# The rotary key projection as one chunk: weights held, x moving, result turned back by TensorE

## The chip, the cores and the metric

The kernel runs on one core of a Trainium2 chip. TensorE (PE) does matrix products and transposes into PSUM, VectorE (DVE) and ScalarE (ACT) work element by element, GpSimd (POOL) does small tables and issues some DMAs, SyncE (SP) issues the weight loads. The metric is the device time in microseconds of one execution, as the median of several runs.

## The reference, cut to what matters

Two decoder layers over 256 tokens of width 2048. Layer 0 is attention with a combined input projection, layer 1 a state-space (S5) layer; each is followed by layer norm, a gated feed-forward part and another layer norm. The part around the change:

```python
q_lat, kv_lat, k_pe, qd, kd, vd = jnp.split(h @ w_in, splits, axis=-1)   # k_pe: 64 columns
q = (_rmsnorm(q_lat, q_norm) @ w_q_b).reshape(B, S, MLA_HEADS, NOPE_DIM + ROPE_DIM)
q = jnp.concatenate([q[..., :NOPE_DIM], _rope(q[..., NOPE_DIM:], positions)], axis=-1)
kv = (_rmsnorm(kv_lat, kv_norm) @ w_kv_b).reshape(B, S, MLA_HEADS, NOPE_DIM + V_DIM)
k_pe = jnp.broadcast_to(_rope(k_pe[:, :, None, :], positions), (B, S, MLA_HEADS, ROPE_DIM))
k = jnp.concatenate([kv[..., :NOPE_DIM], k_pe], axis=-1)
```

So k_pe is x (256 x 2048) times a weight of 2048 x 64, rotated by position, and shared by the eight heads.

## The kernel before, in words

All weights come as "chunks" of two row tiles (2 x 128 rows) and up to 512 columns, 512 KB each. SP loads them one after the other into a ring of four slots, `RAW` (`load`, L250 to L256); a load waits until DVE is done with the chunk four before it (`lo_ready`). A product in full f32 is made of three in fp32r: ACT copies the chunk to `WH`, which keeps the high part (`hi`, L689), DVE writes the rest to `WL` (`lo`, L974), and PE adds up x_hi w_hi, x_hi w_lo and x_lo w_hi (`chunk`, L349 to L351). `hi` and `lo` of chunk c wait until PE has used chunk c - 4 (`w_used`); PE waits for `lo_ready`. In `chunk` a tile of x (128 rows by 128 tokens) is the stationary operand and the weights, 512 columns, are the moving one; the result has the tokens on the partitions. There are 12 matmuls a chunk, 2 row tiles x 2 token tiles x 3.

Each engine runs its own program, whose order is written out by hand and tied together by semaphores. `PHASES` gives each projection its number of blocks, the chunks of a block, the number of its first chunk and of its first block. Blocks alternate between two accumulators `A` in PSUM (`acc_ready` waits for `acc_free`).

The order around the change is: "win" (8 blocks of 8 chunks, chunks 0 to 63), "kpe" (one block, chunks 64 to 71, of width 64, so that each matmul writes 128 x 64 and loads 128 x 128 of x), "qb" (3 blocks of 2 chunks), "kvb" (4 blocks of 2 chunks), then attention, then "wout". In the kpe phase ACT splits five narrow chunks, copies out the last block of win (`win_end(7)`, L725) and splits the other three. DVE, after the first two chunks of qb, waits for the end of kpe, rotates the result straight from PSUM into `STG` (`rotate`, L1032 to L1034, six operations), writes it twice side by side (L1102) and counts `staged`, for which PE's `turn_up(0)` waits. That turns it by two transposes (L414), and DVE copies the turned key to `KP` (`whole_turned`, L986). `Y`, two banks of PSUM, lies unused in this stage.

Of the kernel before, what the change touches and what calls it, by code (L numbers as in the profile page):

```python
# [25 lines left out]
P = 128  # L26
TOK = 256
TT = TOK // P
D = 2048
KT = D // P  # L30
WB = 512
RING = 4
# [3 lines left out]
ROPE = 64  # L36
# [16 lines left out]

PHASES = {}
_c = _b = 0
for _name, _n, _per in [("win", 8, 8), ("kpe", 1, 8), ("qb", 3, 2), ("kvb", 4, 2), ("wout", 4, 8),
                        ("ple0", 4, 1), ("gate0", 4, 8), ("inA0", FA, 8), ("outA0", 4, FA), ("inB0", FB, 8), ("outB0", 4, FB),
                        ("glu", 8, 8),
                        ("ple1", 4, 1), ("gate1", 4, 8), ("inA1", FA, 8), ("outA1", 4, FA), ("inB1", FB, 8), ("outB1", 4, FB)]:
    PHASES[_name] = (_n, _per, _c, _b)  # L60
    _c += _n * _per
    _b += _n if not _name.startswith("ple") else 0
# [20 lines left out]
def build(nc, t, out):  # L83
# [3 lines left out]
    with ExitStack() as ctx:  # L87
# [3 lines left out]
        def sem(name):  # L91
            return ctx.enter_context(nc.semaphore(name))


        RAW = at("raw", [P, RING, 2, WB], 0)
# [94 lines left out]
        turn_done = sem("turn_done")  # L190
        turn_hi = sem("turn_hi")
        turned = sem("turned")
        staged = sem("staged")
        v_step = sem("v_step")
        sq_sum = sem("sq_sum")
        trig = sem("trig")
# [22 lines left out]
        n = 0  # L219
# [21 lines left out]
        def _(sp):  # L241
# [16 lines left out]
            def phase(name, weight, width=WB, first=0):  # L258

                nb, per, c0, _ = PHASES[name]  # L260
                w, total = t[weight], nb * per
                if c0 == 0:
                    for j in range(first):
                        load(w, j, j, 0, None, width)
                        if j < 2:
                            load_x(2 + j)
                if (total - first) % RING:
                    for j in range(first, total):
                        load(w, j, c0 + j, 0, None, width)
                elif total - first == RING:  # L270
                    for j in range(first, total):
                        load(w, j, c0 + j, 0, None, width)
                else:
                    with sp.Fori(0, (total - first) // RING) as i:
                        for j in range(RING):
                            load(w, first + j, c0 + first + j, RING, i, width)
# [41 lines left out]
                    sp.dma_start(TS[n % 10][:], c_dram[n].rearrange("p (a c n) -> p a c n", a=4, c=2)).then_inc(ts_in[n % 10], 16)  # L318

            phase("win", "w_in", first=RING)  # L320
            phase("kpe", "w_kpe", ROPE)
            phase("qb", "w_qb")
            phase("kvb", "w_kvb")
            phase("wout", "w_out")
# [15 lines left out]
        def _(pe):  # L340
            def chunk(c, coef, i, hi, lo, kt, depth, acc, width=WB):

                pe.wait_ge(lo_ready, lin(c + 1, coef, i))
                s = c % RING
                for k in range(2):
                    for q in range(TT):
                        cols = slice(q * P, (q + 1) * P)
                        o = A[:, acc, q, 0:width]
                        pe.matmul(o, hi[:, kt + k, cols], WH[:, s, k, 0:width], start=(kt + k == 0), stop=False)  # L349
                        pe.matmul(o, hi[:, kt + k, cols], WL[:, s, k, 0:width], start=False, stop=False)  # L350
                        last = pe.matmul(o, lo[:, kt + k, cols], WH[:, s, k, 0:width], start=False,  # L351
                                         stop=(kt + k == depth - 1))
                last.then_inc(w_used, 1)
# [28 lines left out]
            for b in range(8):  # L382
                acc_ready(b0 + b)
                for j in range(per):
# [8 lines left out]
                    if j == 3 and 1 <= b <= 6:  # L393
                        pe.wait_ge(staged, b)
                        first = TG["lat"] + 2 * (b - 1) if b <= 2 else TG["qk"] + 2 * (b - 3)
                        for g in range(2):
                            turn(first + g, STG[:, (b - 1) % 2], 256 * g)
            _, per, c0, b0 = PHASES["kpe"]
            acc_ready(b0)
            for j in range(per):  # L400
                chunk(c0 + j, 0, None, XH, XL, 2 * j, KT, b0 % 2, ROPE)


            QB, KVB = PHASES["qb"], PHASES["kvb"]
# [1 line left out]

            def turn_up(m):

                pe.wait_ge(staged, 7 + m)
                if m == 0:  # L410
                    g = TG["kpe"]
                    pe.wait_ge(turned, g - 1)
                    for q in range(TT):
                        last = pe.transpose(TP[:, g % 2, 0, q * P:(q + 1) * P], STG[:, 0, q, 0:P], ID[:])  # L414
                    last.then_inc(turn_done, 1)
                else:
                    for g in range(2):
                        turn(groups[m] + g, STG[:, m % 2], 256 * g)

            pe.wait_ge(turned, TG["qk"])  # L420
            for b in range(7):
                acc_ready(QB[3] + b)
                for j in range(2):
                    row = 2 * j
                    part = slice(0, 4) if b < 3 else slice(4, 8)
                    chunk(QB[2] + 2 * b + j, 0, None, LH[:, part], LL[:, part], row, 4, (QB[3] + b) % 2)
                if b >= 1 and b <= 6:
                    turn_up(b - 1)

# [243 lines left out]
        def _(act):  # L673
# [9 lines left out]
            def hi(c, coef=0, i=None, width=WB):  # L683

                s = c % RING
                act.wait_ge(raw_full[s], lin(16 * (c // RING + 1), 16 * coef // RING, i))
                if c >= RING:
                    act.wait_ge(w_used, lin(c - RING + 1, coef, i))
                act.activation(WH[:, s, :, 0:width], RAW[:, s, :, 0:width], ACT.Copy).then_inc(hi_ready, 1)  # L689
# [20 lines left out]
            def win_end(b):  # L710

                end("win", b)
                if b < 2:
                    if b == 0:
                        act.wait_ge(const_in, 6 * 16)
                    else:
                        act.wait_ge(sq_sum, 2 * b)
                    for q in range(TT):
                        act.activation(GTf[:, WB * q:WB * (q + 1)], A[:, b % 2, q], ACT.Square,
                                       accum_out=SC[:, 2 * b + q:2 * b + q + 1]).then_inc(sq_sum, 1)  # L720
                elif b < 6:
                    act.wait_ge(turn_done, TG["lat"] + 2 * (b - 1))
                    act.activation(STG[:, b % 2], A[:, b % 2], ACT.Copy).then_inc(staged, 1)
                else:
                    act.activation(VD[:, :, (b - 6) * WB:(b - 5) * WB], A[:, b % 2], ACT.Copy).then_inc(acc_free, 1)  # L725
# [17 lines left out]
                            n_ = 2 * (b - 1) + g  # L743
                            hi_turned(TG["lat"] + n_, LH[:, 2 * n_:2 * n_ + 2, :])
            c0 = PHASES["kpe"][2]
            for j in range(8):
                hi(c0 + j, width=ROPE)
                if j == 4:
                    win_end(7)
            QB, KVB = PHASES["qb"], PHASES["kvb"]  # L750

            def up_end(m):
# [206 lines left out]
        def _(dve):  # L959
# [8 lines left out]
            def lo(c, coef=0, i=None, width=WB):  # L968

                s = c % RING  # L970
                dve.wait_ge(hi_ready, lin(c + 1, coef, i))
                if c >= RING:
                    dve.wait_ge(w_used, lin(c - RING + 1, coef, i))
                dve.tensor_tensor(WL[:, s, :, 0:width], RAW[:, s, :, 0:width], WH[:, s, :, 0:width].bitcast(F32),  # L974
                                  ALU.subtract).then_inc(lo_ready, 1)
# [99 lines left out]
                                n_ = 2 * (b - 3) + g  # L1075
                                whole_turned(TG["qk"] + n_, QK[:, 2 * n_:2 * n_ + 2, :])
            c0 = PHASES["kpe"][2]
            for j in range(8):
                lo(c0 + j, width=ROPE)
            QB = PHASES["qb"]  # L1080

            def up_turned(m):
# [9 lines left out]
            for b in range(7):  # L1092
                lo(QB[2] + 2 * b)
                lo(QB[2] + 2 * b + 1)
                if b == 0:

                    end("kpe", 0)
                    src = A[:, PHASES["kpe"][3] % 2, :, 0:ROPE].rearrange("p t (h c n) -> p t h c n", h=1, c=2)
                    dve.wait_ge(turn_done, TG["kpe"])
                    dst = STG[:, 0, :, 0:ROPE].rearrange("p t (h c n) -> p t h c n", h=1, c=2)  # L1100
                    link(rotate(src, dst, 1))
                    link(dve.tensor_copy(STG[:, 0, :, ROPE:2 * ROPE], STG[:, 0, :, 0:ROPE]))  # L1102
                    dve.nop().then_inc(staged, 1)
                    dve.nop().then_inc(acc_free, 1)
                if b in (1, 2, 4, 5):
                    dve.wait_ge(staged, 7 + b)
                    dve.nop().then_inc(acc_free, 1)
                if b == 3:
                    end("qb", 2)
                    dve.wait_ge(turn_done, TG["qn"] + 2)  # L1110
                    src = A[:, (QB[3] + 2) % 2].rearrange("p t (h c n) -> p t h c n", h=HEADS, c=2)
                    dst = STG[:, 1].rearrange("p t (h c n) -> p t h c n", h=HEADS, c=2)
                    link(rotate(src, dst, HEADS))
                    dve.nop().then_inc(staged, 1)
                    dve.nop().then_inc(acc_free, 1)
                if b >= 2:
                    up_turned(b - 2)
# [814 lines left out]
```

## Time and profile before

| | us |
|---|---|
| median of 3 runs | 2473.98 (2472.92 to 2474.0) |
| the profiled execution | 2473.81 |
| its span | 2472.0 |
| PE busy | 2340.4 |
| DVE busy | 1453.1 |
| ACT busy | 1033.2 |
| mean granted clock of PE, of full | 0.971 |

The span is the time from the first to the last instruction of the profiled execution. Busy times of the engines overlap. The durations of neighbouring matmuls overlap too, since they are pipelined; how fast PE goes is read from the distance of their starts. The granted clock has two levels here, 2.4 GHz (1.00) and 1.2 GHz (0.50); a value between them for a stretch is a mean.

### The profile page before, as it was taken

To read this page: it belongs to the slowest core of one execution; us is meant where nothing else is said; L and a number is where in the kernel's file an instruction comes from. 1 tells how busy PE (TensorE), PEld (TensorE's weight loads), DVE (VectorE), ACT (ScalarE), POOL (GpSimd) and SP (SyncE) were. 2 spreads that over 40 slices of the span, in tenths; PEclk is the share of its full clock that TensorE was granted. 3 is DMA by queue.
4 is the path that set the end of the run, shared out by engine and by line. 5 is a ranking of instruction groups with operands and counts; after the bars stand their busy time and mean duration, and the time that the engine had idled before them with its cause. 6 is when DMAs were issued, how large, how long until landed. Compare 5 with 4: busy or idle time off the path is not lost.

```text
span 2472.0 us, 32904 instructions
## 1 busy us (share of the span) xinstructions
PE 2340.4 (95%) x10996; PEld 1927.8 (78%) x10996; DVE 1453.1 (59%) x1924; ACT 1033.2 (42%) x1134; POOL 219.3 (9%) x327
## 2 busy tenths in 40 slices
PE   8999999999999999999948499989999999999996
PEld 6888687888888888888836488868888888888885
DVE  5544757666667776557836755475544444445455
ACT  4443544444444334444333044344444443444442
POOL 0000048501111011101210000000000000000000
PEclk9998999999999999999969799999999999999998
DMA  6554264768787667767685156556555555555553
GB/s 237 186 181 128 87 198 144 234 222 259 256 266 251 227 232 240 240 196 253 228 196 171 51 183 195 171 181 196 192 187 189 189 191 194 191 191 189 188 189 117
DMA packets 136992, 483.02 MB, mean 195 GB/s; under 512 B 18656, under 2 KB 19168, under 8 KB 135744
## 3 DMA queue, kind: packets, MB, share of 16 engines
q1 hardware_dynamic: 121568, 429.44, 53.7%
q0 software_dynamic: 14048, 50.80, 6.8%
q10 hardware_dynamic: 1280, 1.48, 0.2%
q8 instruction: 62, 1.02, 0.2%
q14 instruction: 34, 0.28, 0.0%
HBM read 457.80 MB, written 19.14 MB: 193 GB/s over the span
## 4 chain that ended last, share of the span: by engine, by line
PE 91%; DVE 5%; DMA 2%; issue 1%; ACT 1%; DVEq 0%; SPq 0%; ACTq 0%
PE ps L349 28%; PE ps L350 28%; PE ps L351 28%; PE ps L365 1%; PE ps L628 1%; PE ps L589 1%; DMA h_quarter<-res 1%; DVE w_lo L974 1%; DVE gated L1549 1%; DMA raw<-in_w_in 1%; DVE gated L1547 1%; DMA raw<-in_w_glu 1%; DVE res L1202 0%; ACT w_hi L689 0%; PE ps L448 0%
## 5 line engine op out<-in xcount | busy, mean ns | idle before, releaser
L974 DVE TENSOR_TENSOR w_lo<-raw,w_hi 128x1024 fp32r<-128x1024 f32 (+1 forms) x782 | 951.8, 1220 | 859.7 <-ACT w_hi L689 856.7
L689 ACT ACTIVATE w_hi<-raw 128x1024 fp32r<-128x1024 f32 (+1 forms) x782 | 822.1, 1053 | 1190.3 <-PE ps L351 1152.0
L349 PE MATMUL ps<-w_hi,x_hi 128*128 128x512 f32 (+1 forms) x2336 | 917.0, 393 | 17.9 <-DVE x_lo L982 14.8
L351 PE MATMUL ps<-w_hi,x_lo 128*128 128x512 f32 (+1 forms) x2336 | 910.9, 390 | 0.0
L350 PE MATMUL ps<-w_lo,x_hi 128*128 128x512 f32 (+1 forms) x2336 | 910.5, 390 | 0.0
L349 PEld LDWEIGHTS ps<-w_hi,x_hi 128*128 128x128 f32 x2336 | 442.8, 190 | 109.9 <-DVE x_lo L982 16.7
L351 PEld LDWEIGHTS ps<-w_hi,x_lo 128*128 128x128 f32 x2336 | 442.6, 189 | 91.4
L350 PEld LDWEIGHTS ps<-w_lo,x_hi 128*128 128x128 f32 x2336 | 443.0, 190 | 88.4
L349 PE MATMUL ps<-w_hi,hid_hi 128*128 128x512 f32 x704 | 275.2, 391 | 0.0
L350 PE MATMUL ps<-w_lo,hid_hi 128*128 128x512 f32 x704 | 274.1, 389 | 0.0
L351 PE MATMUL ps<-w_hi,hid_lo 128*128 128x512 f32 x704 | 274.0, 389 | 0.0
L349 PEld LDWEIGHTS ps<-w_hi,hid_hi 128*128 128x128 f32 x704 | 132.1, 188 | 28.7 <-issue 1.4
L351 PEld LDWEIGHTS ps<-w_hi,hid_lo 128*128 128x128 f32 x704 | 132.2, 188 | 27.8
L350 PEld LDWEIGHTS ps<-w_lo,hid_hi 128*128 128x128 f32 x704 | 132.2, 188 | 27.0
L1643 POOL TENSOR_TENSOR s_small<-s_small 64x128 f32<-64x128 f32 x93 | 71.1, 764 | 7.5
L628 PE MATMUL ps<-s_table,states 128*64 128x128 f32 x256 | 32.1, 290 | 39.3 <-DVE states L1551 39.3
L628 PEld LDWEIGHTS ps<-s_table,states 128*64 128x64 f32 x256 | 30.9, 198 | 39.9 <-DVE states L1551 39.5
L577 PE MATMUL ps<-ident,h_steps 64*128 64x64 f32 x64 | 7.8, 314 | 33.8 <-ACT h_steps L894 33.8
L1764 POOL DMA_DIRECT2D s_e_dram<-s_e x16 | 8.9, 558 | 338.2 <-DVE s_e L1342 338.2
L921 ACT ACTIVATE z<-ps 128x512 f32<-128x512 f32 x8 | 4.8, 598 | 81.6 <-PE ps L628 81.6
L1757 POOL DMA_DIRECT2D s_coef<-s_coef_dram x64 | 35.5, 561 | 4.4 <-DMA s_coef_dram<-s_small 4.2
L1261 DVE TENSOR_TENSOR gated<-ps,gated 128x512 f32<-128x512 f32 x44 | 30.2, 685 | 8.5 <-ACT gated L856 8.5
(201 smaller groups left out, 1339.7 us busy)
## 6 DMA issues: line engine op xcount, KB each, us to landing
raw<-in_w_inA SPq DMA_DIRECT2D x192, 512.0 KB, 4.3
raw<-in_w_inB SPq DMA_DIRECT2D x160, 512.0 KB, 4.1
raw<-in_w_outA SPq DMA_DIRECT2D x96, 512.0 KB, 4.3
raw<-in_w_outB SPq DMA_DIRECT2D x80, 512.0 KB, 4.3
raw<-in_w_in SPq DMA_DIRECT2D x64, 512.0 KB, 4.1
raw<-in_w_gate SPq DMA_DIRECT2D x64, 512.0 KB, 4.3
raw<-in_w_glu SPq DMA_DIRECT2D x64, 512.0 KB, 4.3
raw<-in_w_out SPq DMA_DIRECT2D x32, 512.0 KB, 4.3
```

The costliest lines, as they stand in the source:

```text
L349: pe.matmul(o, hi[:, kt + k, cols], WH[:, s, k, 0:width], start=(kt + k == 0), stop=False)
L350: pe.matmul(o, hi[:, kt + k, cols], WL[:, s, k, 0:width], start=False, stop=False)
L351: last = pe.matmul(o, lo[:, kt + k, cols], WH[:, s, k, 0:width], start=False, stop=(kt + k == depth - 1))
L365: last = pe.transpose(TP[:, g % 2, k, q * P:(q + 1) * P], src[:, q, col + k * P:col + (k + 1) * P], ID[:])
L589: last = pe.matmul(PS[0:SLOTS, 2 * (tile % 2) + a // 2, TOK * (a % 2):TOK * (a % 2 + 1)], U4[:, 4 * tile + a, :], TS[tile % 6][:, a].rearr ...
L628: last = pe.matmul(bank_of(pair), ST[:, :, ri, pair], TS[n_ % 10][:, a, ri, :], start=False, stop=(ri == 1), skip_group_check=True)
L689: act.activation(WH[:, s, :, 0:width], RAW[:, s, :, 0:width], ACT.Copy).then_inc(hi_ready, 1)
L974: dve.tensor_tensor(WL[:, s, :, 0:width], RAW[:, s, :, 0:width], WH[:, s, :, 0:width].bitcast(F32), ALU.subtract).then_inc(lo_ready, 1)
L1261: dve.tensor_tensor(GT[:, 1], A[:, bb % 2, :, 256:512], GT[:, 0], ALU.mult).then_inc(hid_ready, 1)
L1547: ins = dve.tensor_tensor(prod[h], abar[:, :, :, m], x.unsqueeze(1).broadcast_to([P, 2, 2, half]), ALU.mult)
L1643: link(pool.tensor_tensor(o, a, b, op))
L1757: pool.dma_start(EC[n][PW * s:PW * (s + 1)].rearrange("p a c n -> p a (c n)"), src).then_inc(e_raw[n], 16)
```

## The change

kpe becomes one chunk of 512 KB that holds all 16 row tiles of the 2048 x 64 weight. Its slices of 64 columns are the stationary operand, and x_hi or x_lo, 256 tokens wide, is the moving one: 16 x 3 = 48 matmuls that write 64 x 256, features on the partitions. DVE copies that to a free part of `STG`, PE transposes it back by two transposes into `Y` after the first chunk of qb (`turn_kpe`), and DVE rotates from there, now after the splits of qb's chunks 3 and 4. The rotations count a semaphore of their own, `rotated`, and the numbers that `staged` is waited for are shifted. Chunks and blocks after kpe keep their order; their chunk numbers are lower by seven.

```diff
-for _name, _n, _per in [("win", 8, 8), ("kpe", 1, 8), ("qb", 3, 2), ...
+for _name, _n, _per in [("win", 8, 8), ("kpe", 1, 1), ("qb", 3, 2), ...
             phase("win", "w_in", first=RING)
-            phase("kpe", "w_kpe", ROPE)
+            c = PHASES["kpe"][2]
+            sp.wait_ge(lo_ready, c - RING + 1)
+            sp.dma_start(RAW[:, c % RING].rearrange("p k n -> p (k n)").rearrange("p (a n) -> p a n", a=KT // 2),
+                         t["w_kpe"].rearrange("a p n -> p a n")).then_inc(raw_full[c % RING], 16)
...
             acc_ready(b0)
-            for j in range(per):
-                chunk(c0 + j, 0, None, XH, XL, 2 * j, KT, b0 % 2, ROPE)
+            pe.wait_ge(lo_ready, c0 + 1)
+            w_hi, w_lo = (w[:, c0 % RING].rearrange("p k n -> p (k n)") for w in (WH, WL))
+            for k in range(KT):
+                o, cols = A[0:ROPE, b0 % 2, 0, 0:TOK], slice(ROPE * k, ROPE * (k + 1))
+                pe.matmul(o, w_hi[:, cols], XH[:, k, :], start=(k == 0), stop=False)
+                pe.matmul(o, w_lo[:, cols], XH[:, k, :], start=False, stop=False)
+                last = pe.matmul(o, w_hi[:, cols], XL[:, k, :], start=False, stop=(k == KT - 1))
+            last.then_inc(w_used, 1)
+
+            def turn_kpe():
+
+                pe.wait_ge(kpe_out, 1)
+                for q in range(TT):
+                    first = WB // 2 + q * P
+                    last = pe.transpose(Y[:, 0, ROPE * q:ROPE * (q + 1)], STG[0:ROPE, 0, 1, first:first + P], ID[0:ROPE, 0:ROPE])
+                last.then_inc(kpe_turned, 1)
...
             def turn_up(m):
 
-                pe.wait_ge(staged, 7 + m)
+                if m in (0, 3):
+                    pe.wait_ge(rotated, m // 3 + 1)
+                else:
+                    pe.wait_ge(staged, 6 + m if m < 3 else 5 + m)
...
                     chunk(QB[2] + 2 * b + j, 0, None, LH[:, part], LL[:, part], row, 4, (QB[3] + b) % 2)
+                    if b == 0 and j == 0:
+                        turn_kpe()
...
             c0 = PHASES["kpe"][2]
-            for j in range(8):
-                hi(c0 + j, width=ROPE)
-                if j == 4:
-                    win_end(7)
+            hi(c0)
+            win_end(7)
...
             c0 = PHASES["kpe"][2]
-            for j in range(8):
-                lo(c0 + j, width=ROPE)
+            lo(c0)
...
                 if b == 0:
-
                     end("kpe", 0)
-                    src = A[:, PHASES["kpe"][3] % 2, :, 0:ROPE].rearrange("p t (h c n) -> p t h c n", h=1, c=2)
                     dve.wait_ge(turn_done, TG["kpe"])
+                    dve.tensor_copy(STG[0:ROPE, 0, 1, WB // 2:WB], A[0:ROPE, PHASES["kpe"][3] % 2, 0, 0:TOK]).then_inc(kpe_out, 1)
+                    dve.wait_ge(kpe_out, 1)
+                    dve.nop().then_inc(acc_free, 1)
+                if b == 1:
+                    dve.wait_ge(kpe_turned, 1)
+                    src = Y[:, 0, 0:TT * ROPE].rearrange("p (t h c n) -> p t h c n", t=TT, h=1, c=2)
                     dst = STG[:, 0, :, 0:ROPE].rearrange("p t (h c n) -> p t h c n", h=1, c=2)
                     link(rotate(src, dst, 1))
                     link(dve.tensor_copy(STG[:, 0, :, ROPE:2 * ROPE], STG[:, 0, :, 0:ROPE]))
-                    dve.nop().then_inc(staged, 1)
-                    dve.nop().then_inc(acc_free, 1)
+                    dve.nop().then_inc(rotated, 1)
                 if b in (1, 2, 4, 5):
-                    dve.wait_ge(staged, 7 + b)
+                    dve.wait_ge(staged, 6 + b if b < 3 else 5 + b)
```

## Rows read from the trace of the kernel before

**Rows 1.** The page: PE's busy line, and the chain that ended last by engine.

```profile
PE 2340.4 (95%) x10996; PEld 1927.8 (78%) x10996; DVE 1453.1 (59%) x1924; ACT 1033.2 (42%) x1134; POOL 219.3 (9%) x327
...
PE 91%; DVE 5%; DMA 2%; issue 1%; ACT 1%; DVEq 0%; SPq 0%; ACTq 0%
```

**Rows 2.** Busy time by stretches, around kpe; columns in the first line.

```profile
core 0: us, PE busy (x) PEld busy (x) DVE busy (x) ACT busy (x) POOL busy (x), PEclk, DMA share, GB/s
...
199.93:205.20 5.27, 5.27 (x49) 5.26 (x48) 1.17 (x4) 2.15 (x5) 0.00 (x0) 1.00 0.42 123
205.20:215.44 10.24, 10.24 (x50) 10.24 (x50) 2.74 (x3) 3.48 (x4) 0.00 (x0) 0.50 0.74 240
215.44:218.90 3.46, 3.46 (x9) 2.78 (x10) 2.70 (x8) 1.06 (x1) 0.00 (x0) 0.50 0.09 37
```

**Rows 3.** PE in order of time: start, duration, line, out<-in, stationary, out.

```profile
199.93 0.19 PE L349 MATMUL ps<-w_hi,x_hi 128*128 128x64 f32 x1
...
205.21 0.40 PE L349 MATMUL ps<-w_hi,x_hi 128*128 128x64 f32 x1
...
215.44 0.77 PE L349 MATMUL ps<-w_hi,lat_hi 128*128 128x512 f32 x1
...
218.95 0.39 PE L351 MATMUL ps<-w_hi,lat_lo 128*128 128x512 f32 x1
```

**Rows 4.** Weight loads of L349 (0 to 460 us) and L589: ns minimum/median/maximum.

```profile
L349 PEld LDWEIGHTS ps<-w_hi,x_hi x470: 186/188/333, 12.0 to 459.9; 128*128 128x128 f32 x157
...
L589 PEld LDWEIGHTS ps<-s_table,u x128: 132/137/231, 1293.8 to 1333.9; 128*64 128x64 f32 x128
```

**Rows 5.** An S5 stage with 64 weight columns: PE's order, and a stretch.

```profile
1299.86 1.94 PE L589 MATMUL ps<-s_table,u 128*64 128x256 f32 x8
1301.73 0.71 PE L603 MATMUL ps<-ident,e_slots 64*128 64x64 f32 x8
...
1300.00:1310.00 10.00, 10.00 (x65) 6.30 (x65) 4.04 (x4) 4.03 (x5) 0.00 (x0) 1.00 0.72 218
```

**Rows 6.** PE in order of time around two transposes of L414.

```profile
227.79 0.40 PE L351 MATMUL ps<-w_hi,lat_lo 128*128 128x512 f32 x1
228.03 0.38 PE L414 MATMUL ps<-ident,stage 128*128 128x128 f32 x2
...
228.48 0.39 PE L350 MATMUL ps<-w_lo,lat_hi 128*128 128x512 f32 x1
```

**Rows 7.** ACT and DVE in order of time; in brackets idle time before and releaser.

```profile
189.31 1.06 ACT L689 ACTIVATE w_hi<-raw 128x1024 fp32r<-128x1024 f32 x1 [1.66 <-PE ps L351]
192.03 0.31 ACT L689 ACTIVATE w_hi<-raw 128x128 fp32r<-128x128 f32 x1 [1.66 <-PE ps L351]
...
201.67 1.01 ACT L725 ACTIVATE v_dil<-ps 128x1024 f32<-128x1024 f32 x1
...
190.40 1.23 DVE L974 TENSOR_TENSOR w_lo<-raw,w_hi 128x1024 fp32r<-128x1024 f32 x1 [1.49 <-ACT w_hi L689]
...
215.67 0.23 DVE L1032 TENSOR_TENSOR gated<-ps,cos_sin 128x64 f32<-128x64 f32 x1 [2.75 <-PE ps L351]
...
229.67 0.42 DVE L986 COPY k_pe<-ps 128x256 f32<-128x256 f32 x1 [2.53 <-ACT stage L762]
```

**Rows 8.** SP's issues of kpe, and DMA issues with us to landing.

```profile
183.64 17.91 SPq L256 DMA_DIRECT2D raw<-in_w_kpe  x8
...
raw<-in_w_in SPq DMA_DIRECT2D x4, 512.0 KB, 4.0
...
raw<-in_w_kpe SPq DMA_DIRECT2D x8, 64.0 KB, 2.2
```

**Rows 9.** PE in attention, the same step of three heads in order of time.

```profile
282.87 1.22 PE L465 MATMUL ps<-probs_t,v_dil 128*128 128x256 f32 x2
...
287.92 0.70 PE L465 MATMUL ps<-probs_t,v_dil 128*128 128x256 f32 x2
...
290.99 0.70 PE L465 MATMUL ps<-probs_t,v_dil 128*128 128x256 f32 x2
```

More of the change, by code:

```diff
@@ L55 @@
 _c = _b = 0
-for _name, _n, _per in [("win", 8, 8), ("kpe", 1, 8), ("qb", 3, 2), ("kvb", 4, 2), ("wout", 4, 8),
+for _name, _n, _per in [("win", 8, 8), ("kpe", 1, 1), ("qb", 3, 2), ("kvb", 4, 2), ("wout", 4, 8),
                         ("ple0", 4, 1), ("gate0", 4, 8), ("inA0", FA, 8), ("outA0", 4, FA), ("inB0", FB, 8), ("outB0", 4, FB),
@@ L192, in build @@
         turned = sem("turned")
-        staged = sem("staged")
+        staged, rotated, kpe_out, kpe_turned = sem("staged"), sem("rotated"), sem("kpe_out"), sem("kpe_turned")
         v_step = sem("v_step")
@@ L397, in _ @@
                             turn(first + g, STG[:, (b - 1) % 2], 256 * g)
-            _, per, c0, b0 = PHASES["kpe"]
+            _, _, c0, b0 = PHASES["kpe"]
             acc_ready(b0)
-            for j in range(per):
-                chunk(c0 + j, 0, None, XH, XL, 2 * j, KT, b0 % 2, ROPE)
+            pe.wait_ge(lo_ready, c0 + 1)
[12 more added lines that the diff above has]
+                last.then_inc(kpe_turned, 1)
             QB, KVB = PHASES["qb"], PHASES["kvb"]
@@ L1113, in _ @@
                     link(rotate(src, dst, HEADS))
-                    dve.nop().then_inc(staged, 1)
+                    dve.nop().then_inc(rotated, 1)
                     dve.nop().then_inc(acc_free, 1)
```

## The prediction

> **What bounds the kernel now.** I read the page first. TensorE (PE) is busy 95% of the span, and the chain that ended last is 91% PE and 5% VectorE (DVE) [rows 1]. So, outside a few places, a microsecond taken from PE's stream is a microsecond of the span, and work of ScalarE (ACT), DVE or the DMA queue matters only where PE comes to wait for it. The granted clock by stretches comes second. The rotary key projection ("kpe") starts at 199.93; PE is busy in all of it, yet from 205.20 its clock is at half rate, 1.2 instead of 2.4 GHz, until 218.90, well into the query projection ("qb") that follows [rows 2]. Third, PE's order of time gives the intervals between starts, which is what counts, since the durations of neighbours overlap [rows 3]:
>
> - 48 of the 96 narrow matmuls (64 columns out) run from 199.93 to 205.21, 0.11 us each; the other 48, at the half clock, from 205.21 to 215.44, 0.213 us each. Together 15.51 us.
> - The first 8 matmuls of qb, of 512 columns, take from 215.44 to 218.95, 3.51 us. At full clock the next 39, up to 227.79 [rows 6], take 8.84 us, 0.2267 each, so those eight would be 1.81 us.
>
> PE has no idle time anywhere in these rows: nobody feeds it too late, it is slow by itself.
>
> **Why narrow matmuls cost so much.** 64 columns at one a cycle are 27 ns of 2.4 GHz, but the interval is 111 ns. Two readings fit. (a) The weight load sets it: each narrow matmul has to load 128 columns of x. A load of 128 columns stands in the trace with a median of 188 ns, one of 64 columns with 137 ns [rows 4], so 64 columns more cost 51 ns and 128 cost some 102, nearly the whole interval. (b) A narrow fp32r matmul streams at a quarter of the wide one's rate: 4 x 64 cycles are 107 ns. Both double at the half clock. I take (a), because of what the clock does: it falls after 5.3 us of this stage although PE shows as busy without a gap [rows 2, 3], as it would with an array that streams in only a quarter of its cycles, and it stays at full in a stage of the S5 layer, where matmuls with 64 weight columns stream 256 columns at length [rows 5].
>
> **The change, part by part.** The sum is made against the profiled execution, 2473.81 us (span 2472.0 and 1.8 around it); the median of the runs is 2473.98, 0.2 above.
>
> 1. *The projection on PE.* 96 matmuls of 64 columns with 128 weight columns each go; 48 come, with 64 weight columns (51 ns of load) and 256 moving. No row has this form in fp32r. Nearest below: the 512-wide ones at 0.2267 us take 544 cycles of 2.4 GHz, so they stream one column a cycle, and 256 columns cannot go below 0.107. Nearest above: the plain-f32 form of the same size, 128x64 weights and 256 columns, one record each 0.234 us (eight from 1299.86 to 1301.73) [rows 5]. I take the lower side, since type and buffers are those of the 512-wide row: its 0.2267 less 512 columns at 2.4 GHz (0.2133) leaves 0.0134 of overhead a matmul, and 0.1067 + 0.0134 = 0.120. 48 x 0.120 = 5.76 us; the bounds are 5.1 and 11.2.
> 2. *The clock.* The new stream fills 256 of 288 cycles, so I expect full rate all through: the eight slow qb matmuls become 1.81 us. The doubt is that only 64 of 128 array columns work; the S5 rows with 64 weight columns stay at 1.00 all the same [rows 5].
> 3. *Turning back.* Two PE transposes are added after qb's first chunk. Two such, from L414, stretch the step from 227.79 to 228.48 to 0.69 us where two matmuls would take 0.45: +0.24 us [rows 6]. The two old transposes of the rotated key stay.
> 4. *Who must be in time for PE.* Weights of kpe: its load is issued at 183.64 as before, when the slot is free [rows 8]. It is one of 512 KB in 1024 pieces of 512 bytes instead of eight of 64 KB in 256 pieces of 256 bytes. The old one lands after 2.2 us and a full chunk in 4 KB pieces after 4.0 [rows 8]; four times 2.2 is 8.8, so it is there by 192.4 at the latest. The ACT copy that may start at 192.03 becomes 1.06 us (189.31) instead of 0.31 and the DVE difference 1.23 (190.40) [rows 7], ending by 194.8; PE wants it at 199.93. Cost nothing, with 5 us of cover, and the loads behind it on SP's queue have more.
>    On ACT, the copy-out of the last "win" block (1.01 us, at 201.67 before [rows 7]) now stands in front of the splits of all qb chunks, and waits for PE's end of win: about 200.2 to 201.2. Then the first qb chunk: ACT to 202.3, DVE to 203.5; the second to 204.7. PE wants the first at 199.93 + 5.76 = 205.7. This is the tightest cover, 2.2 us. It was nothing before, when the narrow stage gave 15.5 us. If it failed, PE would wait at the start of qb by just the difference.
>    On DVE, the new copy PSUM to STG of 64x256 comes after the stage's end, some 205.95; the row of a 128x256 copy says 0.42 us [rows 7], so about 206.4. Behind it on DVE stand the differences of chunks three and four of qb (to 207.7 and 208.9) and PE wants these at 211.4 and later. PE's new wait for that copy stands before qb's second chunk and everything behind it, but is reached only at 208.4: 2.0 us of cover. The accumulator is freed right after the copy, also in time. DVE's wait for the turned key (about 208.9) holds the rotation, six operations and a copy that start at 215.67 now and take 0.23 us each, say 0.25 with what lies between [rows 7], until about 210.8; PE asks for the result only after two more chunks, at 216.9, and DVE's next difference waits for ACT until 213.7 anyway. Nothing.
> 5. *Removed off the path.* Seven small ACT copies and seven small DVE differences, and seven DMA issues. They lie beside a busy PE: nothing gained.
>
> Sum over what is replaced: before 15.51 + 3.51 = 19.02; after 5.76 + 1.81 + 0.24 = 7.81. Gain 11.2 us, 2473.98 - 11.2 = **2462.8 us**. Later work is released by PE's progress, so it all moves earlier; I found no timer of its own: POOL's S5 preparation and the SP loads wait for PE's or DVE's counts.
>
> 5a. *What the Trainium skill would make of it.* "TensorE: Matmul & The Clock Gate", section "LDWEIGHTS (loading the stationary operand)", gives a load as its columns / 1.2 in ns: 107 for 128 columns, 53 for 64. That agrees with the 51 ns step of the rows and with reading (a). The same page, "Back-to-back issue gap", puts a full-clock gap at N/2.4 + 2.5 ns, 109 for 256 columns; as an estimate from it the stage would be 5.2 us and the time 2462.3. Its 216 ns for 512 columns is below the measured 226.7, so I stay with the rows.
>
> **What moves besides.** The stages after this one have low-activity places where the clock falls and recovers. In attention one head takes from 282.87 to 287.92, 5.05 us, at the half clock, and the next one 3.07 to 290.99 [rows 9]. Such dips need not fall on the same heads once all is 11 us earlier. I price that by two heads' difference, 2 x 2 us, as +-4 us on any outcome.
>
> **Rivals.**
>
> A. *The clock falls in the new stage too*, since half the array's columns idle. For: it fell after 5.3 us in the old one, and the new one lasts 5.8. Against: the S5 rows. Price: the last 4 matmuls at double interval +0.4 and qb's start slow as now, +1.7, so 2464.9; if it fell halfway, 24 x 0.107 + 1.7 = 4.3, 2467.1.
>
> B. *256 columns of fp32r at two cycles each*, as a record of the plain-f32 form shows: 0.234 x 48 = 11.2 us, 5.5 more than forecast, 2468.3. For: same shape. Against: another type, and the 512-wide fp32r rows run at one.
>
> C. *Reading (b) holds, and 256 is still "narrow"*: four cycles a column. 0.427 + 0.005 = 0.432 each, 20.7 us; or, by two records of the f32 form, 0.468 and 22.5 us. After: 22.8 to 24.5 against 19.02, 3.7 to 5.5 us slower, 2477.7 to 2479.5. This is the case on the other side; it turns from gain to loss where one matmul costs over (19.02 - 1.81 - 0.24)/48 = 0.354 us. For: the 64-wide interval fits it to 5 ns. Against: the falling clock.
>    "FP8 and Floating Point Precision" of the Trainium skill, section "TensorE Precision Notes", says that true FP32 takes four passes through the array. The rows of the 512-wide fp32r form have one; if the narrow form had four, that is case C with its times.
>
> D. *It doesn't do what it says:* PE waits for a late feed at qb's start and takes back what it won. For: cover there shrinks to 2.2 us. Against: it is still cover; a stall of over 6 us would be needed to reach "no difference". I give it little.
>
> **How the numbers follow.** The forecast, full clock and about 0.12 us each: 74%, 2462.8 with 2458.5 to 2467. A: 10%. B: 5%. C: 5%. D, and dips further on that are worse or better than +-4 us: 6%. The range takes in A, most of B and the lower side of the dips: 2458 to 2468.5, leaving out C, the rest of D and the tails. About 0.2%, 5 us, is what a measurement of this kernel can tell from no change. Faster by more: 74 + 10 + 4 of B + 3 of the rest = 0.91. Within: 1 of B, 2 of C, 3 of the rest = 0.06. Slower by more: 3 of C = 0.03.
>
> **What would show it.** In the profile of the changed kernel: 48 matmuls 128*64 with 64x256 out, intervals 0.11 to 0.12 and the stage over at about 205.7; a granted clock of 1.00 from 200 to 240; the first qb matmul at 0.23 intervals and no idle time before it; two transposes at about 208.4 with no wait for the DVE copy; the rotation from about 209; qb beginning at 205.7 and everything after it 11 us earlier. An interval of 0.23 shows B, 0.43 or more C; a clock of 0.5 at qb's start A; idle time before qb released by the DVE difference D. If these stand and the total is off by several us, the difference must be found where the clock dips in later stages, and my ignorance of those is what is likeliest to spoil the figure.

## The result

The changed kernel takes 2462.66 us (median of 6 runs, 2458.5 to 2463.01), beside 2473.99 for the kernel before in the same comparison (6 runs, 2469.99 to 2478.03). The ratio is 0.9949, with an interval of 0.9939 to 0.9959: about 0.5% or 12.6 us faster by the ratio, 11.3 by the two medians. The prediction was 2462.8.

The profile after was taken of the quickest of the six executions (2458.5 us, span 2456.7), so it shows more than the change alone. The page of the changed kernel, the lines that answer to [rows 1]:

```profile
span 2456.7 us, 32749 instructions
...
PE 2323.5 (95%) x10950; PEld 1912.6 (78%) x10950; DVE 1452.3 (59%) x1918; ACT 1030.9 (42%) x1127; POOL 220.3 (9%) x327
...
PE 90%; DVE 5%; DMA 2%; issue 1%; ACT 1%; DVEq 0%; SPq 0%; ACTq 0%
```

PE is the bound as before; its busy time fell by 16.9 us, DVE's and ACT's hardly. Next its order of time around kpe, to be held against [rows 3] and [rows 6] (L407 to L409 are the new matmuls, L417 the turning back, L352 to L354 the old `chunk`):

```profile
199.76 0.28 PE L407 MATMUL ps<-x_hi,w_hi 128*64 128x256 f32 x1
...
205.09 0.28 PE L409 MATMUL ps<-x_lo,w_hi 128*64 128x256 f32 x1
205.20 0.40 PE L352 MATMUL ps<-w_hi,lat_hi 128*128 128x512 f32 x1
...
207.04 0.39 PE L354 MATMUL ps<-w_hi,lat_lo 128*128 128x512 f32 x1
...
207.72 0.39 PE L354 MATMUL ps<-w_hi,lat_lo 128*128 128x512 f32 x1
208.04 0.34 PE L417 MATMUL ps<-ident,stage 64*128 64x64 f32 x2
208.31 0.50 PE L352 MATMUL ps<-w_hi,lat_hi 128*128 128x512 f32 x1
208.65 0.39 PE L353 MATMUL ps<-w_lo,lat_hi 128*128 128x512 f32 x1
```

The 48 matmuls take 5.44 us, from 199.76 to 205.20, 0.1133 each, with an even step; the first eight of qb follow in 1.84 us (to 207.04) without idle time. The stretches that answer to [rows 2], with the same columns, show the full clock all through:

```profile
199.90:205.70 5.80, 5.80 (x52) 5.71 (x50) 2.66 (x3) 4.11 (x5) 0.00 (x0) 1.00 0.25 75
205.70:215.00 9.30, 9.30 (x42) 7.41 (x41) 5.67 (x12) 3.75 (x4) 0.00 (x0) 1.00 0.56 179
```

ACT and DVE in order of time, for [rows 7]:

```profile
199.96 1.03 ACT L747 ACTIVATE v_dil<-ps 128x1024 f32<-128x1024 f32 x1 [7.04 <-PE ps L354]
200.88 2.95 ACT L711 ACTIVATE w_hi<-raw 128x1024 fp32r<-128x1024 f32 x3
...
201.96 2.36 DVE L994 TENSOR_TENSOR w_lo<-raw,w_hi 128x1024 fp32r<-128x1024 f32 x2 [7.79 <-ACT w_hi L711]
205.41 0.42 DVE L1117 COPY stage<-ps 64x256 f32<-64x256 f32 x1 [1.08 <-PE ps L409]
206.04 2.36 DVE L994 TENSOR_TENSOR w_lo<-raw,w_hi 128x1024 fp32r<-128x1024 f32 x2 [0.21 <-DVE stage L1117]
208.41 0.22 DVE L1052 TENSOR_TENSOR gated<-ps,cos_sin 128x64 f32<-128x64 f32 x1
```

ACT waits 7.04 us for the end of win and only then begins with qb's chunks, as foreseen; DVE has the first ready near 203.2, 2 us before PE begins with it at 205.20. The copy of the result is done at 205.83, 2.2 us before the transposes. Last, the one load of kpe, beside [rows 8]:

```profile
raw<-in_w_kpe SPq DMA_DIRECT2D x1, 512.0 KB, 4.5
```

Attention starts at 250.94, before at 262.31 (L443's first matmul). Of these 11.37 us the stages ahead of kpe, which the change leaves alone, are 0.17 (199.93 against 199.76); 11.20 are the change's, against the execution before that the rows were read from. Another profile of the kernel before gives more, see the section after the experiments.

### The profile page after: what moved, and what is told of

The parts are those of the page before. It is cut to its first block, busy times and chain, and to the rows that moved or that the text cites. A ratio compares the mean times of both kernels' runs of the same rounds, so it can differ in the third digit from the quotient of the medians.

```text
span 2456.7 us, 32749 instructions
## 1 busy us (share of the span) xinstructions
PE 2323.5 (95%) x10950; PEld 1912.6 (78%) x10950; DVE 1452.3 (59%) x1918; ACT 1030.9 (42%) x1127; POOL 220.3 (9%) x327
## 4 chain that ended last, share of the span: by engine, by line
PE 90%; DVE 5%; DMA 2%; issue 1%; ACT 1%; DVEq 0%; SPq 0%; ACTq 0%
PE ps L352 28%; PE ps L354 28%; PE ps L353 28%; PE ps L368 1%; PE ps L650 1%; PE ps L611 1%; DVE w_lo L994 1%; DMA h_quarter<-res 1%; DMA raw<-in_w_in 1%; DVE gated L1571 1%; DVE gated L1569 1%; DMA raw<-in_w_glu 1%; DVE res L1224 0%; ACT w_hi L711 0%; PE ps L625 0%
## 5 line engine op out<-in xcount | busy, mean ns | idle before, releaser
L994 DVE TENSOR_TENSOR w_lo<-raw,w_hi 128x1024 fp32r<-128x1024 f32 x775 | 950.4, 1229 | 850.1 <-ACT w_hi L711 847.3
L711 ACT ACTIVATE w_hi<-raw 128x1024 fp32r<-128x1024 f32 x775 | 820.4, 1060 | 1173.7 <-PE ps L354 1135.3
L352 PE MATMUL ps<-w_hi,x_hi 128*128 128x512 f32 x2304 | 905.7, 393 | 18.5 <-DVE x_lo L1002 15.1
L354 PE MATMUL ps<-w_hi,x_lo 128*128 128x512 f32 x2304 | 899.4, 390 | 0.0
L353 PE MATMUL ps<-w_lo,x_hi 128*128 128x512 f32 x2304 | 899.0, 390 | 0.0
L352 PEld LDWEIGHTS ps<-w_hi,x_hi 128*128 128x128 f32 x2304 | 434.2, 188 | 109.3 <-DVE x_lo L1002 17.0
L354 PEld LDWEIGHTS ps<-w_hi,x_lo 128*128 128x128 f32 x2304 | 433.9, 188 | 91.4
L353 PEld LDWEIGHTS ps<-w_lo,x_hi 128*128 128x128 f32 x2304 | 434.3, 189 | 88.7
L352 PE MATMUL ps<-w_hi,hid_hi 128*128 128x512 f32 x704 | 275.2, 391 | 0.0
L354 PE MATMUL ps<-w_hi,hid_lo 128*128 128x512 f32 x704 | 274.0, 389 | 0.0
L352 PEld LDWEIGHTS ps<-w_hi,hid_hi 128*128 128x128 f32 x704 | 132.1, 188 | 28.6 <-issue 1.4
L354 PEld LDWEIGHTS ps<-w_hi,hid_lo 128*128 128x128 f32 x704 | 132.2, 188 | 27.7
L1569 DVE TENSOR_TENSOR gated<-a_bar,states 128x128 f32<-128x128 f32 x124 | 32.1, 288 | 5.0 <-ACT states L937 1.9
```

The source lines that it names most:

```text
L1569: ins = dve.tensor_tensor(prod[h], abar[:, :, :, m], x.unsqueeze(1).broadcast_to([P, 2, 2, half]), ALU.mult)
```

## Experiments

The theory, L: a narrow matmul costs the load of its weight columns, and the clock falls because little streams through the array, although PE shows as busy. The rival, S: under some width fp32r streams at a quarter of the rate. The prediction had chosen L on the clock's word; a width of 256 that comes out well fits both, if S's width lies under it.

**Half the moving columns.** `e1_move128`: twice the matmuls, the same loads each.

```diff
-                o, cols = A[0:ROPE, b0 % 2, 0, 0:TOK], slice(ROPE * k, ROPE * (k + 1))
-                pe.matmul(o, w_hi[:, cols], XH[:, k, :], start=(k == 0), stop=False)
+                cols = slice(ROPE * k, ROPE * (k + 1))
+                for r in range(2):
+                    m = slice(TOK // 2 * r, TOK // 2 * (r + 1))
+                    o = A[0:ROPE, b0 % 2, 0, m]
+                    pe.matmul(o, w_hi[:, cols], XH[:, k, m], start=(k == 0 and r == 0), stop=False, skip_group_check=True)
...
```

> The changed kernel, but each of its 48 matmuls of kpe is cut in two of 128 moving columns (96 in all, 64 weight columns each). Theory L (the 0.111 us of the old narrow matmuls was the load of 128 weight columns): a load of 64 columns is about 0.051 us and 128 columns stream in 0.053, so an interval of 0.055 to 0.067 and a stage of 5.3 to 6.4 us, about as now (5.44), full clock, total within 1 us of 2462.7. Theory S (fp32r under some width streams at a quarter of the rate): 0.21 to 0.22 us each, 20 to 21 us for the stage, some 2478.

It took 2461.72 us (2 runs), ratio 0.9947 (0.9927 to 0.9967). PE in order of time:

```profile
199.72 0.22 PE L410 MATMUL ps<-x_hi,w_hi 128*64 128x128 f32 x1
...
205.48 0.45 PE L352 MATMUL ps<-w_hi,lat_hi 128*128 128x512 f32 x1
```

96 matmuls in 5.76 us, 0.060 each. That is as many matmuls as the kernel before had, at about half the full-clock price of its narrow ones, with twice as many columns moving. S's 0.21 is out for 128 columns.

**A quarter.** `e2_move64` cuts in four, 192 matmuls of 64 moving columns, the very width of the old ones.

> As before it but cut in four of 64 moving columns (192 matmuls, 64 weight columns). L: bound by the load of 64 columns, 0.051 to 0.06 us each, stage 9.8 to 11.5 us at full clock, total about 2468; the array streams in half of its cycles, so the clock may fall near the end. S: 0.111 us each as in the kernel before, stage 21 us, some 2478.

One run, 2465.76 us. PE in order of time:

```profile
199.77 0.19 PE L410 MATMUL ps<-x_hi,w_hi 128*64 128x64 f32 x1
...
210.94 0.48 PE L352 MATMUL ps<-w_hi,lat_hi 128*128 128x512 f32 x1
```

11.17 us for 192, 0.058 each: the same interval as with 128 moving columns. So it is not the stream that sets it. The operands have changed places against the old form, but both forms move 64 columns of fp32r; the size that differs is the number of weight columns, 64 for 128, and the interval differs by a factor of 1.9 (0.111 us in the old form). Theory S is refuted at 64 columns too, where it was made to fit.

**The old form, twice as wide.** `e3_old_width128` is the kernel before, where each matmul of kpe writes 128 instead of 64 columns (the second half multiplies stale weights and is never read).

```diff
-                chunk(c0 + j, 0, None, XH, XL, 2 * j, KT, b0 % 2, ROPE)
+                chunk(c0 + j, 0, None, XH, XL, 2 * j, KT, b0 % 2, 2 * ROPE)
```

> The kernel before, with PE's matmuls of kpe 128 instead of 64 columns wide (the second half multiplies stale weights and is never read; loads, splits and the rest as before). L: interval still the load's 0.111 us at full clock; and if the clock falls for want of streaming columns, it falls later or not at all, since twice as many stream: stage 10.7 us with qb at full clock right after (some 2467), or at worst as before, 2474. S: 0.22 us each at full clock, stage 21 us, about 2477, and the clock does not fall.

One run, 2470.99 us. Stretches of it, columns as in [rows 2]; the first is just the stage:

```profile
200.25:210.92 10.67, 10.67 (x97) 10.66 (x96) 3.91 (x7) 4.97 (x9) 0.00 (x0) 1.00 0.63 209
210.92:214.00 3.08, 3.08 (x16) 2.51 (x16) 2.35 (x8) 1.74 (x2) 0.00 (x0) 1.00 0.84 267
```

This kernel does twice the arithmetic in kpe and the stage is 4.8 us shorter, 10.67 against 15.51, since the interval stays at 0.111 and the clock never falls, neither there nor at qb's start. Nothing differs from the kernel before but the columns that stream through the array between two loads. That bears out both halves of L. Twice the moving columns leave the interval as it is, and with e2 that makes it the load's. And the clock that fell with 64 moving columns stayed up with 128, at the same interval and with PE busy without a gap in both, so it went by what streams and not by waiting (one profile of this kernel; the fall stands in both profiles of the kernel before). Attention starts at 256.2, 6 us earlier than before; the total is only 3 us shorter, mainly because this profile's attention was a slow one (54.3 us for 49.6, see the section after this one).

**One chunk without the swap.** `e4_one_chunk_old_form` undoes the heart of the change and keeps the rest: one load, one split, but x held and 64 weight columns moving, and no turning back.

```diff
-                pe.matmul(o, w_hi[:, cols], XH[:, k, :], start=(k == 0), stop=False)
+                for q in range(TT):
+                    o, m = A[:, b0 % 2, q, 0:ROPE], slice(P * q, P * (q + 1))
+                    pe.matmul(o, XH[:, k, m], w_hi[:, cols], start=(k == 0), stop=False)
...
```

> The change without the swap: one chunk of 512 KB, but x is the stationary operand and the 64 weight columns move, 96 matmuls, and DVE rotates straight from PSUM as before; no turning back. If the gain is all in the swapped form (my reckoning), this takes 2474 us, the clock falls as before, kpe and the slow start of qb take 19.0 us. If fewer chunks and waits were the gain, it is near 2463.

2474.82 us (10 runs), ratio 1.0001 (0.9991 to 1.0011): no difference. Its stretches from the start of kpe:

```profile
199.79:203.60 3.81, 3.81 (x36) 3.81 (x35) 1.61 (x2) 3.61 (x4) 0.00 (x0) 1.00 0.00 0
203.60:215.60 12.00, 12.00 (x59) 12.00 (x58) 0.76 (x1) 0.25 (x1) 0.00 (x0) 0.50 0.27 87
215.60:220.60 5.00, 5.00 (x15) 4.14 (x16) 3.22 (x9) 1.06 (x1) 0.00 (x0) 0.50 0.00 0
```

Fewer chunks, waits and DMA issues are worth nothing that these runs can tell, as they lay beside a busy PE. The clock falls here too, after 3.8 us where it had been 5.3; kpe and the slow start of qb are 20.8 us instead of the 19.0 expected. That is no price of the one chunk: from the start of kpe to qb's 48th matmul it takes 29.52 us, and the repeated profile of the kernel before, where the clock also falls early, 29.49 (27.86 in the first).

**Eating up the cover.** `e5b_act_delay` puts four more copies on ACT ahead of qb's chunks.

```diff
+                    for _ in range(4 if b == 7 else 0):
+                        act.activation(VD[:, :, (b - 6) * WB:(b - 5) * WB], A[:, b % 2], ACT.Copy).then_inc(padded, 1)
+                        act.wait_ge(padded, _ + 1)
                     act.activation(VD[:, :, (b - 6) * WB:(b - 5) * WB], A[:, b % 2], ACT.Copy).then_inc(acc_free, 1)
```

> The changed kernel with four more copies of the last win block on ACT, each waited for, between win_end(7)'s wait and its own copy (the same data written again). It tests the cover reckoned for qb's first chunk: in the changed kernel DVE has it ready about 2.0 us before PE asks (205.20). Four copies of 1.03 us with their waits are 4.4 to 4.6 us, so PE should stand idle before qb for 2.3 to 2.6 us, released by the DVE difference, and the total be 2.4 us longer, 2465. If the cover were larger, no idle time; if the whole delay showed, 4.5 us.

2465.05 us (4 runs), ratio 0.9958 (0.9943 to 0.9974); the changed kernel in the same comparison took 2461.93, so 3.1 us more. PE in order of time, and one stretch:

```profile
205.28 0.28 PE L409 MATMUL ps<-x_lo,w_hi 128*64 128x256 f32 x1
207.77 0.47 PE L352 MATMUL ps<-w_hi,lat_hi 128*128 128x512 f32 x1 [2.21 <-DVE w_lo L997]
```

```profile
209.00:212.00 3.00, 3.00 (x8) 2.08 (x7) 2.44 (x3) 0.20 (x1) 0.00 (x0) 0.50 0.88 287
```

qb starts at 207.77 where 205.39 (205.28 and one interval) would have done: 2.38 us late, released by the DVE difference. Of a delay of 4.2 us (four copies, 200.15 to 204.39) the cover took what had been reckoned, about 2, and the rest went straight into the span. What was not expected: after the pause the clock drops for some 3 us (second fence), which no profile of the changed kernel shows there. Some eight matmuls then take 0.427 us instead of 0.227, 1.6 us in all, so that a late feed costs more than its length; attention starts at 255.1, 1.3 to 1.8 us later than those 2.4 explain. This is one profile.

**High and low part side by side.** Since 128 columns load in 0.111 us, just under the 0.1133 that 256 take to stream, the stage has room for twice the weight columns. `e6_hi_lo_side_by_side` uses it, with two thirds of the matmuls.

```diff
+        W2 = at("w_both", [P, KT, 2, ROPE], 176, F32R)
+        I2 = at("ident2", [P, ROPE], 191)
...
+                both = W2[:, k].rearrange("p a n -> p (a n)")
+                pe.matmul(A[:, b0 % 2, 0, 0:TOK], both, XH[:, k, :], start=(k == 0), stop=False)
+                last = pe.matmul(A[:, b0 % 2, 0, 0:TOK], both, XL[:, k, :], start=False, stop=(k == KT - 1))
...
+                    last = pe.matmul(Y[:, 0, ROPE * q:ROPE * (q + 1)], STG[:, 0, 1, first:first + P], I2[:],
+                                     start=True, stop=True)
```

> A step further: ACT and DVE write w_hi and w_lo of each row tile side by side, so 128 weight columns are held, and x_hi and x_lo each move once over them: 32 matmuls of 256 columns instead of 48 (it adds the product lo x lo). The two halves of the result are added by PE in the turning back, as a matmul with two identities stacked; ACT splits qb's first chunk before it copies out the last win block. Theory L: 128 columns load in 0.102 to 0.111 us, just under the 0.1134 us of 256 streaming, so still 0.113 to 0.12 each, the stage 3.6 to 3.9 instead of 5.44 us, tail about as now: 1.6 to 1.9 us faster than the changed kernel, 2461. If load and stream do not fully overlap at these sizes: 0.15 us or more each, 4.8 us, 0.6 us gained. The clock stays full.

2459.2 us (5 runs), ratio 0.9935 (0.9921 to 0.9948). PE in order of time:

```profile
200.01 0.28 PE L408 MATMUL ps<-x_hi,w_both 128*128 128x256 f32 x1
...
203.84 0.40 PE L354 MATMUL ps<-w_hi,lat_hi 128*128 128x512 f32 x1
```

3.83 us for 32 matmuls, 0.1197 each, 6 ns more than with 64 weight columns: load and stream overlap almost fully. The stage gains 1.61 us. Its turning back, two plain matmuls in four records behind the same wait for DVE's copy, shows the weight loads without idle time:

```profile
206.36 0.39 PE L356 MATMUL ps<-w_hi,lat_lo 128*128 128x512 f32 x1
206.59 0.55 PE L417 MATMUL ps<-ident,stage 128*128 128x64 f32 x4
206.95 0.48 PE L354 MATMUL ps<-w_hi,lat_hi 128*128 128x512 f32 x1
207.27 0.39 PE L355 MATMUL ps<-w_lo,lat_hi 128*128 128x512 f32 x1
```

The step is 0.91 us where two matmuls take 0.45: 0.46 for four loads of 128 columns that run on end. In the changed kernel the row of the two loads has idle time before it:

```profile
208.04 0.20 PEld L417 LDWEIGHTS ps<-ident,stage 64*128 64x128 f32 x2 [0.35 <-issue]
```

That kernel and the changed one were timed again side by side, `e10_side_by_side_rounds` and `e9_after_rounds`.

> The changed kernel, timed beside the next one on the same chip: 0.995 of the kernel before, some 11 to 13 us, by reckoning 11.2 of it up to the start of attention.

> The kernel with w_hi and w_lo side by side once more, on the same chip as the changed one: by its profile the stage is 1.6 us shorter, so it should come out 1 to 2 us below the changed kernel; a larger difference would belong to the executions, not to the edit.

The changed kernel came to 2461.93 us (5 runs, 2458.93 to 2462.64), ratio 0.9945 (0.9931 to 0.9958); the further one to 2456.96 (5 runs, 2456.35 to 2458.98), ratio 0.9931 (0.9917 to 0.9945). Here the difference is 5.0 us by the medians and 3.5 by the two ratios. The edit explains 1.6 us of it; the rest is not explained by anything in kpe. The next section shows where such amounts come and go.

## How much belongs to an execution

`e7_after_again` and `e8_before_again` are the two kernels once more, with a profile.

> The changed kernel once more, profiled, to see what of its time belongs to an execution and not to the change: up to the start of attention it should repeat to 0.3 us (250.9); in attention and S5 the granted clock may dip elsewhere and give 1 to 6 us more.

> The kernel before once more, profiled. The fall of the clock in kpe should be there again; it may come earlier or later than 5.3 us into the stage, by which the stage and qb's start differ by up to some 2 us. Attention and S5 as in the other profiles, 48 to 54 us and 151 to 153.

They took 2461.71 and 2472.54 us. The changed kernel repeats: from the start of kpe to qb's 48th matmul it takes 16.64 us in each of its three profiles. The kernel before does not, for its clock falls at another moment. From its repeated profile, PE in order of time:

```profile
204.17 0.36 PE L350 MATMUL ps<-w_lo,x_hi 128*128 128x64 f32 x1
...
216.07 0.77 PE L349 MATMUL ps<-w_hi,lat_hi 128*128 128x512 f32 x1
...
221.32 0.39 PE L349 MATMUL ps<-w_hi,lat_hi 128*128 128x512 f32 x1
```

The clock falls at 204.17, 4.4 us into the stage instead of 5.3, and is back at 221.32 instead of 218.95; up to qb's 48th matmul it is 29.49 us instead of 27.86, and attention starts at 263.80. So against this execution the change gives 12.9 us (29.49 less 16.64), against the first 11.2. Further on neither kernel repeats. The stretch from the first attention matmul to the first of "wout", columns as in [rows 2], in six profiles, one fence each: the kernel before, the same again, the changed one, the same again, a third time (`e9_after_rounds`), and the side-by-side kernel (`e10_side_by_side_rounds`).

```profile
262.31:311.90 49.59, 44.49 (x208) 32.12 (x209) 41.75 (x131) 31.04 (x100) 0.00 (x0) 0.90 0.20 66
```

```profile
263.80:312.50 48.70, 43.18 (x209) 31.28 (x209) 41.54 (x131) 30.99 (x100) 0.00 (x0) 0.93 0.19 66
```

```profile
250.94:298.80 47.86, 40.64 (x209) 29.21 (x209) 41.49 (x131) 30.77 (x100) 0.00 (x0) 1.00 0.20 68
```

```profile
251.40:299.10 47.70, 40.61 (x208) 29.20 (x209) 41.33 (x131) 30.81 (x100) 0.00 (x0) 1.00 0.20 68
```

```profile
251.30:305.50 54.20, 49.10 (x207) 35.16 (x208) 41.74 (x131) 31.07 (x100) 0.00 (x0) 0.81 0.17 59
```

```profile
249.40:298.00 48.60, 41.82 (x209) 30.45 (x209) 41.61 (x131) 30.94 (x100) 0.00 (x0) 0.96 0.20 67
```

The same kernel has an attention of 47.7 or 54.2 us, by whether the clock dips in it. Over all twelve profiles it was 47.7 to 54.3, with mean clocks from 1.00 to 0.81. The part from there to the S5 layer varied from 963.1 to 966.4 us, the S5 part from 150.5 to 153.5, and what follows it hardly (1041.4 to 1042.2). A single profile or run can therefore not tell an edit of a few microseconds; the timed comparisons and the stage itself can. That the first profile after was 15.3 us shorter in its span than the one before is made up of 11.4 up to attention, 1.7 in attention, and the remaining 2.2 behind it.

## Why the prediction was right, point by point

1. *What bounds.* PE, by its own stream. Right: removing chunks and waits alone is worth nothing (e4), and the earlier start arrives at attention in full, 11.20 us by the profile against 11.2 reckoned from the same execution.
2. *Why the narrow matmuls were dear.* Reading (a), taken on the argument of the clock, is now shown and not only argued: 0.058 us with 64 weight columns and 64 moving (e2), 0.111 with 128 weight columns and either 64 or 128 moving (before, e3). Case B and case C are out by the 0.1133 us of the changed kernel, and reading (b) by e2: even 64 columns do not stream at a quarter of the rate. "TensorE: Matmul & The Clock Gate" of the Trainium skill, section "LDWEIGHTS (loading the stationary operand)", gives 53 and 107 ns for these loads; the intervals in the runs, 58 and 111 ns, agree within 5 ns.
3. *The projection.* Forecast 5.76 us, measured 5.44. The overhead that I took over from the 512-wide matmul, 13 ns each, was too much; it is 7 ns (0.1133 less 256 columns at 2.4 GHz, 0.1067). It goes by the weight columns and not by the moving ones: 7 ns as well with 64 weight and 128 moving columns (e1, 0.060 less 0.0533), and 13 again with 128 weight and 256 moving (e6, 0.1197 less 0.1067), as in the 512-wide row, which also has 128. The term was 0.32 us too high.
4. *The clock.* Forecast to stay at full; in the stage it did, in every profile of the swapped form, and at qb's start in all but e5b, behind its pause. It is the larger part of the gain: at full clock the old matmuls take 10.67 us (e3, same interval), so 4.84 of the 10.07 us that the stage lost, and 1.67 of qb's start, are the clock's; 5.23 us are the halved loads.
5. *Turning back.* Forecast +0.24 us from two 128x128 transposes [rows 6]; measured 0.48, as the step from 207.72 to 208.65 is 0.93 where two matmuls take 0.45. The two transposes read 64 partitions, and the weight loads show 0.35 us of idle time before them. The wait for DVE's copy, fulfilled some 2 us earlier, does not do that by itself: e6 has the same wait fulfilled as early, and its loads run without idle time (it pays 0.46 us, but for four loads instead of two). What is left is the form, 64 partitions in transposes; it was not tried alone. The step was mis-sized by a factor of two, and it is luck that it just about cancels the error in point 3.
6. *Cover.* The load landed after 4.5 us, not the 8.8 at the upper bound; qb's first chunk had 2 us of cover, as e5b confirms from the other side. Case D's price was too low: in e5b the stall was followed by a slow clock, which the case had not counted.
7. *Sum.* 10.07 + 1.67 - 0.48 = 11.26, measured up to attention 11.20. The timed medians differ by 11.3 and the ratios of two comparisons stand for 12.6 and 13.6 us. The sum was made against one execution of the kernel before, the one whose clock fell latest in the three profiles with 64 moving and 128 weight columns (5.3 us into the stage; 4.4 in e8, 3.8 in e4); against e8 the same change is 12.9 us. So the term of 19.02 us for kpe and qb's start holds for that execution and not for every one, and a good part of the 1 to 2 us above the sum can lie there; how the timed runs are spread over such moments is not known. That the median came out within 0.2 us of the forecast is in part luck. One guess was in the prediction, that dips of the clock in later stages move; the table shows that they do, but not that they move in favour of the change.

## What to carry to other kernels

Where a matmul has one small side, hold the small side as the weights and move the large one: the load costs by weight columns (64: 0.058 us, 128: 0.111), and moving columns are free until their stream is longer than the load. A narrow stage with PE busy at 100% can still lose half of its clock; look at the granted clock and at the start intervals before believing the busy share, and look at the stage behind it too, which pays for the recovery. Where a clock falls at a moment that varies, read more than one profile before pricing it. If the clock falls, even useless columns can pay for themselves (e3), but the swap is better.

## What the runs showed of the hardware

- Matmul intervals in fp32r at full clock, weight columns x moving columns: 64 x 64, 0.058 us; 64 x 128, 0.060; 64 x 256, 0.1133; 128 x 64 and 128 x 128, 0.111; 128 x 256, 0.1197; 128 x 512, 0.2267. Where the moving columns set the interval, it is their number at 2.4 GHz and 7 ns with 64 weight columns, 13 ns with 128.
- PE busy without a gap, 128 weight columns: with 64 moving columns an interval the clock went to 1.2 GHz after 3.8 to 5.3 us; with 128 it stayed at 2.4 GHz for the whole 10.67 us. With 64 weight and 64 moving columns, at the shorter interval of 0.058 us, it also stayed, for 11.2 us.
- A pause of 2.2 us on PE was followed, 1 us after work had begun again, by some 3 us at the half clock (e5b, one profile); together they cost more than the pause.
- The changed form took 16.64 us from the start of kpe to qb's 48th matmul in three profiles of three; the old one 27.86 and 29.49, by the moment at which the clock fell.
